# The opening of a two-block kernel by feature columns, with the low part's product of the first projection one chunk later

## The chip, the core and the metric

The kernel runs on one core of one Trainium2 chip. The metric is the device time of one execution in microseconds (us). The engines are TensorE (PE; its weight loads are PEld), VectorE (DVE), ScalarE (ACT), GpSimd (POOL) and SyncE (SP), which here only issues transfers. Each engine works through its own queue in order; between engines there are semaphores.

## What is computed

Two blocks follow each other on x (1 x 1024 tokens x 1024 features, fp32). The first has two layers of attention and SwiGLU with adaLN modulation, the second an SSM and a short convolution. Only the first lines of the first layer matter here:

```python
cond = silu(c)
mod = cond @ ada_w[0] + ada_b[0]
sh1, sc1, g1, sh2, sc2, g2 = split(mod, 6)
h = rmsnorm(x, norm_mix[0]) * (1 + sc1) + sh1
qkv = h @ a_w_in[0]          # 16 query heads, 4 key/value heads of 64
```

`rmsnorm` divides each token by the root of the mean of its squares (plus 1e-6) and multiplies by a gain per feature.

## The kernel before

**The data.** h is kept with features on partitions: eight chunks k of 128 features x 1024 tokens. Every matrix product is split: h and the weight tile are each cut into a high part (fp32r) and a low part (what is left), and a product is three matmuls: high weight x high h (L1500), high weight x low h (L1501), low weight x high h (L1502). A tile of a weight is 128 partitions x 1024. ScalarE makes its high part (`tile_highs`, L2531), VectorE its low part (`tile_lows`, L3592). Attention runs in units; unit 0 needs the three tiles kv, q0 and q1, each for two halves of 512 tokens.

**The opening.** SyncE loads vec, c, the eight token tiles of x (`x_start`, L998), the kv tile and then the adaLN weights of chunk 0 to 7 (`ada_start`, L1003, 1 MB each, six places), with q0 behind chunk 1 and q1 behind chunk 5. ScalarE squares the token tiles with its accumulator (`square_tile`, L2612; VectorE does the last, L3618). VectorE and ScalarE make the factor per token in two groups of four tiles (`factor_of`, `root_of`) and scale x by it, four tiles each (`scale_tile`). TensorE spreads silu(c) over the partitions (L1554), runs 12 spare products (`spare_products`, L1431) and turns x chunk by chunk into PSUM (`turn_x`, L1546), up to three chunks ahead.

**The chunk loop.** For each chunk VectorE takes two products of a 128x1024 adaLN tile with silu(c), summed over the row (`modulation`, L2892), which give shift and scale, then the gain (L3638); ScalarE writes h from the turned x with gain and shift (L2638) and its high part (L2641); VectorE writes the low part of the chunk before (`first_low`, L3630). TensorE's `project_first` waits for that low part (`h_ready`) and runs kv and q0 of the chunk, 12 products; the 48 products of q1 come in one piece behind chunk 7, with the turn of the values (`turn_values`, L1571) ahead of its chunk 6. Then `attention` goes on: VectorE copies keys and values out of PSUM (L3418, L3420), ScalarE the queries, SyncE loads unit 1's kv tile when a place is free (L872), and TensorE alternates scores (L1593) with the projection of unit 1.

**GpSimd** builds identity, distances and the ALiBi tables of units 0 and 1 (`bias_tables`, L1148), and then waits for unit 0's projection to issue adaLN loads (L1162).

The order is written out by hand on each engine. The spare products and the first lines of the projection read:

```python
def spare_products(n, dst=psum[:, 3584:3840]):
    for _ in range(n):
        nc.tensor.matmul(dst, ident[:, :], pick[:, 0:2, :], start=True, stop=True)
```

## Time and profile before

| | us |
|---|---|
| median of 3 runs | 2569.73 (2568.26 to 2569.94) |
| profiled execution, its own time | 2567.95 |
| its span | 2565.9 |
| TensorE busy | 2529.6 (99%) |
| VectorE busy | 1970.2 (77%) |
| ScalarE busy | 1035.0 (40%) |
| GpSimd busy | 321.0 (13%) |

The page gives busy times and a chain of waits. Behind it stand views of the trace: instructions in order of time (merged where equal ones follow each other, so that the second number is the time from the first start to the last end), the chain in order of time, one line's instructions, and busy times by stretch. An fp32 matmul leaves two records, an fp32r one leaves one. Ends of matmuls are modelled, so the time of one is read from start to start.

### The profile page before, as it was taken

What the parts mean: (1) busy time and instruction counts of PE and PEld (TensorE: products, weight loads), DVE (VectorE), ACT (ScalarE), POOL (GpSimd) and SP (SyncE); (2) the same over time, 40 slices, a digit from 0 to 9 for tenths busy, and PEclk for the clock granted to TensorE, in tenths of its full rate; (3) what the DMA queues carried; (4) which work ended last, traced back from release to release, by engine and by line L of the source; (5) the groups of instructions that cost most, each with busy time, mean ns of one, the idle gap of its engine ahead of it and who ended that gap; (6) DMA issues with size and microseconds to landing.
All of it is one profiled execution on the core that took longest, in us unless ns stands there. A gap on an engine that the chain in (4) does not pass through costs nothing.

```text
span 2565.9 us, 37223 instructions
## 1 busy us (share of the span) xinstructions
PE 2529.6 (99%) x12662; PEld 2018.7 (79%) x12662; DVE 1970.2 (77%) x3476; ACT 1035.0 (40%) x1946; POOL 321.0 (13%) x454
## 2 busy tenths in 40 slices
PE   8999999999999999999999999999999999999998
PEld 6666688888888888777776888888888888878987
DVE  7888757889999889845555888998999987433566
ACT  6445725343333333454446453333333343111233
POOL 2011101000000000301111200000000017971000
PEclk9999999999999999999999999999999999999999
DMA  6333231211111111222322112121111132113122
GB/s 239 116 139 124 99 107 54 62 54 61 49 53 53 57 57 45 90 84 94 99 99 108 40 43 62 50 61 57 49 57 55 59 83 74 50 42 60 34 99 82
DMA packets 182017, 192.61 MB, mean 75 GB/s; under 512 B 18353, under 2 KB 146577, under 8 KB 181490
## 3 DMA queue, kind: packets, MB, share of 16 engines
q1 hardware_dynamic: 169954, 147.48, 18.0%
q0 software_dynamic: 11952, 43.65, 5.4%
q8 instruction: 69, 1.13, 0.2%
q14 instruction: 42, 0.34, 0.0%
HBM read 177.34 MB, written 12.58 MB: 74 GB/s over the span
## 4 chain that ended last, share of the span: by engine, by line
PE 93%; DVE 4%; ACT 2%; issue 1%; DMA 1%; POOL 0%; SPq 0%; DVEq 0%
PE psum L1423 21%; PE psum L1730 10%; PE psum L1731 10%; PE psum L1732 10%; PE psum L1500 5%; PE psum L1783 4%; PE psum L1782 4%; PE psum L1786 4%; PE psum L1502 4%; PE psum L1501 4%; PE psum L1771 3%; PE psum L1593 3%; PE psum L1621 3%; PE psum L1605 3%; DVE arena L2892 1%
## 5 line engine op out<-in xcount | busy, mean ns | idle before, releaser
L3181 DVE SCALAR_TENSOR_TENSOR xT<-psum,mod,xT 128x512 f32<-128x512 f32 x504 | 356.4, 745 | 61.6 <-PE psum L1786 61.3
L2346 ACT ACTIVATE w_high<-wpair 128x512 fp32r<-128x512 f32 x240 | 146.5, 626 | 315.8 <-DVE wpair L3113 244.9
L1423 PE MATMUL psum<-hT_high,w_low 128*128 128x512 f32 x928 | 261.0, 392 | 0.2 <-DVE arena L2888 0.2
L2549 ACT ACTIVATE arena<-arena 128x256 f32<-128x256 f32 (+3 forms) x296 | 146.6, 497 | 157.3 <-DVE arena L3451 157.1
L1500 PE MATMUL psum<-hT_high,w_low 128*128 128x512 f32 x480 | 203.0, 423 | 3.4 <-DVE h_low_mix L3630 3.2
L1423 PEld LDWEIGHTS psum<-hT_high,w_low 128*128 128x128 f32 x928 | 172.9, 188 | 38.3 <-issue 2.5
L1502 PE MATMUL psum<-hT_high,w_low 128*128 128x512 f32 x480 | 189.3, 394 | 0.0
L1501 PE MATMUL psum<-h_low_mix,w_low 128*128 128x512 f32 x480 | 188.5, 393 | 0.0
L1732 PE MATMUL psum<-hT_high,w_low 128*128 128x512 f32 x480 | 186.7, 389 | 0.0
L1730 PE MATMUL psum<-hT_high,w_high 128*128 128x512 f32 x472 | 183.6, 389 | 0.0
L1731 PE MATMUL psum<-h_low,w_high 128*128 128x512 f32 x472 | 183.6, 389 | 0.0
L3099 DVE TENSOR_TENSOR w_low<-wpair,w_high 128x512 fp32r<-128x512 f32 x240 | 161.8, 682 | 2.1 <-ACT w_high L2346 1.7
L1223 POOL TENSOR_TENSOR w_high<-arena,w_high 128x512 fp32r<-128x512 f32 x2 | 2.6, 1292 | 1233.9 <-ACT w_high L2333 1233.9
L3592 DVE TENSOR_TENSOR w_low<-wpair,w_low 128x1024 fp32r<-128x1024 f32 x70 | 88.6, 1267 | 85.5 <-ACT w_low L2531 85.4
L1782 PE MATMUL psum<-hT_high,w_low 128*128 128x512 f32 x360 | 140.1, 389 | 0.0
L1423 PE MATMUL psum<-h_low_mix,w_low 128*128 128x512 f32 x448 | 135.3, 390 | 0.2 <-ACT arena L2273 0.2
L1500 PEld LDWEIGHTS psum<-hT_high,w_low 128*128 128x128 f32 x480 | 90.4, 188 | 57.1 <-issue 36.3
L2531 ACT ACTIVATE w_low<-wpair 128x1024 fp32r<-128x1024 f32 x76 | 80.0, 1054 | 130.6 <-DMA wpair<-in_w_in_dram 94.1
L2562 ACT ACTIVATE arena<-psum 128x1024 f32<-128x1024 f32 (+2 forms) x80 | 85.2, 1066 | 87.8 <-PE psum L1605 87.7
L3451 DVE CUSTOM_DVE_ANT_0 arena<-psum,arena 128x192 f32<-128x192 f32 (+2 forms) x180 | 53.8, 353 | 86.0 <-PE psum L1593 86.0
L2392 ACT ACTIVATE arena<-psum 128x512 f32<-128x512 f32 x80 | 47.9, 599 | 170.3 <-PE psum L1732 114.6
L3113 DVE TENSOR_TENSOR wpair<-wpair 128x512 f32<-128x512 f32 x160 | 109.9, 687 | 6.6
(450 smaller groups left out, 6257.5 us busy)
## 6 DMA issues: line engine op xcount, KB each, us to landing
wpair<-in_ffn_w_in_dram SPq DMA_DIRECT2D x176, 256.0 KB, 2.9
wpair<-in_ada_tiles_dram POOLq DMA_DIRECT2D x20, 1024.0 KB, 5.2
arena<-in_ffn_w_out_dram SPq DMA_DIRECT2D x80, 256.0 KB, 2.9
wpair<-in_ada_tiles_dram POOLq DMA_DIRECT2D x32, 512.0 KB, 3.6
wpair<-in_w_in_dram SPq DMA_DIRECT2D x24, 512.0 KB, 3.8
wpair<-in_b_tiles_dram SPq DMA_DIRECT2D x18, 512.0 KB, 3.3
arena<-in_ada_tiles_dram SPq DMA_DIRECT2D x8, 1024.0 KB, 15.6
wpair<-in_a_tiles_dram SPq DMA_DIRECT2D x12, 512.0 KB, 4.6
```

The costliest lines, as they stand in the source:

```text
L1423: mm = nc.tensor.matmul(dst[:, HALF * a:HALF * a + HALF], w(k), src(k)[:, HALF * t:HALF * t + HALF], start=first and n == 0 and w is high ...
L1500: nc.tensor.matmul(dst, high[:, k, :], hT_high[:, k, rows], start=k == 0, stop=False)
L1501: nc.tensor.matmul(dst, high[:, k, :], h_low_mix[:, k, rows], start=False, stop=False)
L1502: mm = nc.tensor.matmul(dst, low[:, k, :], hT_high[:, k, rows], start=False, stop=k == KC - 1)
L1730: nc.tensor.matmul(bank[dst], high[:, k, :], moving_high(k), start=start and k == 0, stop=False, skip_group_check=not start)
L1731: nc.tensor.matmul(bank[dst], high[:, k, :], moving_low(k), start=False, stop=False, skip_group_check=not start)
L1732: mm = nc.tensor.matmul(bank[dst], low[:, k, :], moving_high(k), start=False, stop=k == 3, skip_group_check=not start)
L1782: nc.tensor.matmul(dst, down_high[w][:, cols], hid_high[v], start=start, stop=False, skip_group_check=not start)
L2346: nc.scalar.activation(of_step(s, first_high, part_high)[name], part_raw[name], ACT.Copy).then_inc(part_high_ready, 1)
L2549: e = nc.scalar.activation(s, s, ACT.Exp, bias=stat_n[:, ti, h:h + 1], scale=-1.0, accum_out=stat_l[:, ti, h:h + 1])
L3099: nc.vector.tensor_tensor(part_low[name], part_raw[name], as_f32(high), ALU.subtract).then_inc(part_split, 1)
L3181: nc.vector.scalar_tensor_tensor(xT[:, m, rows], psum[:, HALF * j:HALF * j + HALF], mod[:, l, 40 + m:41 + m], xT[:, m, rows], ALU.mult, AL ...
```

## The change

x is loaded from its transposed copy `x_rows`, which the kernel already had, so features are on partitions from the start (`x_raw`). The turning of x and the scaling by token tile are gone. ScalarE squares each chunk without its accumulator (VectorE half of the last); TensorE sums the squares over features with one-column products (`square_sums`, eight per chunk), 14 spare products follow, then it spreads the factor over partitions (`factor_wide`, `r_spread`), and 26 more spare products. ScalarE copies the spread factor to `r_wide`. GpSimd multiplies each chunk by it (`scaled`; VectorE does half of chunk 0) and also makes the low parts of kv, q0 and q1 of unit 0. ScalarE writes h and its high part both straight from `x_raw`. In the projection both products with the high part of h run first, the one with the low part a chunk later, and q1 of chunks 0 to 4 runs inside the loop. The q1 load stands behind ada chunk 2.

```diff
-            for t in range(ST):
-                sp.dma_start(x_start[:, t, :], x[0, P * t:P * t + P, :]).then_inc(x_moved[t], 16)
+            for k in range(KC):
+                sp.dma_start(x_raw[:, k, :], x_columns[:, k, :]).then_inc(x_moved[k], 16)
...
-                if k in (1, 5):
+                if k in (1, 2):
                     load_mix("q0" if k == 1 else "q1", 0)
...
+            def tile_lows(name):
+                whole, high, low = tile_parts(name)
+                pool.wait_ge(tile_high, SPLITS.index(name) + 1)
+                pool.wait_ge(tile_split, SPLITS.index(name))
+                nc.gpsimd.tensor_tensor(low, whole, as_f32(high), ALU.subtract).then_inc(tile_split, 1)
+            def scaled(k, first=0):
+                pool.wait_ge(x_moved[k], 16)
+                nc.gpsimd.tensor_tensor(x_raw[:, k, first:S], x_raw[:, k, first:S], r_wide[:, first:S], ALU.mult).then_inc(scaled_ready, 1)
...
             bias_tables(0)
+            tile_lows(("kv", 0))
+            pool.wait_ge(r_kept, 2)
+            scaled(0, HALF)
+            scaled(1)
+            tile_lows(("q0", 0))
+            scaled(2)
+            tile_lows(("q1", 0))
+            for k in range(3, KC):
+                scaled(k)
             bias_tables(1)
...
                 for k in range(KC):
-                    if u == 0:
-                        for n in range(k + 2 if k else 0, min(k + 3, KC)):
-                            turn_x(n)
-                    pe.wait_ge(h_ready, h_number(2 * UNITS[u].layer, k))
+                    pe.wait_ge(shifted, shift_number(0, k))
                     for what in ("kv", "q0"):
+                        with_highs(what, k)
+                    for n in ((k - 1, k) if k == KC - 1 else (k - 1,)):
+                        if n >= 0:
+                            pe.wait_ge(h_ready, h_number(0, n))
+                            for what in ("kv", "q0"):
+                                with_lows(what, n)
+                    if 2 <= k < KC - 1:
                         for half in range(2):
-                            project_chunk(u, what, half, k, first_place(what, half))
-                for k in range(KC):
-                    if k == 6:
+                            project_chunk(u, "q1", half, k - 2, first_place("q1", half))
+                for k in range(5, KC):
+                    if k == KC - 1:
                         turn_values(u)
                     for half in range(2):
                         project_chunk(u, "q1", half, k, first_place("q1", half))
...
+            def square_sums(k):
+                pe.wait_ge(x_squared, k + 1 if k < KC - 1 else KC + 1)
                 for t in range(ST):
+                    mm = nc.tensor.matmul(psum[:, 3584 + t:3585 + t], square_place[k % 2][:, P * t:P * t + P], ones[:, :],
+                                          start=first, stop=k == KC - 1, skip_group_check=t > 0)
+                mm.then_inc(first_norm, 1)
...
+            for k in range(KC):
+                square_sums(k)
+            pe.wait_ge(const_ready, 6)
+            spare_products(14, psum[:, 2560:2816])
+            factor_wide()
+            spare_products(26, psum[:, 2560:2816])
...
+                act.wait_ge(x_moved[k], 16)
+                if k >= 2:
+                    act.wait_ge(first_norm, k - 1)
+                nc.scalar.activation(square_place[k % 2][:, first:S], x_raw[:, k, first:S], ACT.Square).then_inc(x_squared, 1)
...
+                act.wait_ge(scaled_ready, k + 1)
+                nc.scalar.activation(xT[:, k, :], x_raw[:, k, :], ACT.Identity, bias=shift_, scale=gain_)
+                nc.scalar.activation(hT_high[:, k, :], x_raw[:, k, :], ACT.Identity, bias=shift_, scale=gain_).then_inc(shifted, 1)
...
+            dve.wait_ge(first_norm, KC - 1)
+            last = x_raw[:, KC - 1, 0:HALF]
+            nc.vector.tensor_tensor(square_place[1][:, 0:HALF], last, last, ALU.mult).then_inc(x_squared, 1)
...
+                    if k == 0 and b == 0:
+                        dve.wait_ge(r_kept, 1)
+                        nc.vector.tensor_tensor(x_raw[:, 0, 0:HALF], x_raw[:, 0, 0:HALF], r_wide[:, 0:HALF], ALU.mult)
...
-                if k == 0:
-                    tile_lows(("kv", 0))
-                else:
+                if k > 0:
                     first_low(k - 1)
-                if k == 1:
-                    tile_lows(("q0", 0))
```

TensorE's queue from the spread of silu(c) (L1554, in the changed kernel L1600) to the first transposes (`turn_x`, L1546), before:

```order
L1554 MATMUL psum<-arena,ones 128x512
L1431 MATMUL psum<-pick,ident 128x256 [waits x_squared,const_ready]
L1431 MATMUL psum<-pick,ident 128x256 x11
L1546 MATMUL psum<-ident,arena 128x128 [waits scaled_ready,cond_ready]
L1546 MATMUL psum<-ident,arena 128x128 x7
```

and now, from the sums of the last chunk (L1583) on, which seven pairs like it precede, to the first projection product (L1533):

```order
L1583 MATMUL psum<-ones,arena 128x1 [waits x_squared]
L1583 MATMUL psum<-ones,arena 128x1 x7
L1447 MATMUL psum<-pick,ident 128x256 [waits const_ready]
L1447 MATMUL psum<-pick,ident 128x256 x13
L1591 MATMUL psum<-ident,rst 128x128 [waits rstd_ready]
L1591 MATMUL psum<-ident,rst 128x128 x7
L1447 MATMUL psum<-pick,ident 128x256 x26
L1533 MATMUL psum<-hT_high,w_low1 128x512 [waits tile_split,shifted,cond_ready]
```

The spread of the factor stands between two runs of spare products, and the first projection product behind both.

GpSimd's queue from the end of the distance tables on, before:

```order
L1134 AFFINE_SELECT arena<-arena 128x384 [waits pool_step]
L1136 AFFINE_SELECT arena<-arena 128x384 [waits pool_step]
L1148 TENSOR_SCALAR arena<-arena 128x384 [waits pool_step]
L1148 TENSOR_SCALAR arena<-arena 128x384 x7
L1162 DMA wpair2<-in_ada_tiles_dram 128x2x1024 [waits proj_ready1]
```

and now (L1150 is `bias_tables`, L1157 `tile_lows`, L1162 `scaled`; rows of L1162 for chunks 4 to 7 follow, then the tables of unit 1):

```order
L1150 TENSOR_SCALAR arena<-arena 128x384 x3
L1157 TENSOR_TENSOR w_low1<-wpair1,w_low1 128x1024 [waits tile_split,tile_high]
L1162 TENSOR_TENSOR arena<-arena 128x512 [waits x_moved0,r_kept]
L1162 TENSOR_TENSOR arena<-arena 128x1024 [waits x_moved1]
L1157 TENSOR_TENSOR w_low0<-wpair0,w_low0 128x1024 [waits tile_split,tile_high]
L1162 TENSOR_TENSOR arena<-arena 128x1024 [waits x_moved2]
L1157 TENSOR_TENSOR w_low2<-wpair2,w_low2 128x1024 [waits tile_split,tile_high]
L1162 TENSOR_TENSOR arena<-arena 128x1024 [waits x_moved3]
```

Eleven tensor_tensor instructions have come in ahead of the tables of unit 1.

## Rows read from the trace of the kernel before

**Rows 1.** Page of the profile, its first line.

```profile
span 2565.9 us, 37223 instructions
```

**Rows 2.** Chain of waits in order of time, the opening: start us, us, what.

```profile
14.56 1.21 DVE xT L3618
...
17.64 0.46 DVE arena L3609
...
19.49 1.20 DVE arena L2892
...
22.10 1.14 DVE w_low L3592
...
45.68 1.13 DVE h_low_mix L3630
...
49.42 1.15 DVE h_low_mix L3630
```

**Rows 3.** Instructions in order of time, TensorE, the opening: start us, us, what.

```profile
3.98 3.75 PE L1554 MATMUL psum<-arena,ones 1*128 1x512 f32 x4 [3.98 <-ACT arena L2603]
...
27.03 0.50 PE L1500 MATMUL psum<-hT_high,w_low 128*128 128x512 f32 x1 [2.54 <-DVE h_low_mix L3630]
...
54.14 0.39 PE L1500 MATMUL psum<-hT_high,w_low 128*128 128x512 f32 x1
...
64.11 0.39 PE L1502 MATMUL psum<-hT_high,w_low 128*128 128x512 f32 x1
...
64.43 0.71 PE L1571 MATMUL psum<-ident,arena 64*128 64x64 f32 x8
...
68.67 0.50 PE L1500 MATMUL psum<-hT_high,w_low 128*128 128x512 f32 x1
```

**Rows 4.** Instructions in order of time, TensorE, the spare products: whole, then two stretches.

```profile
11.67 8.13 PE L1431 MATMUL psum<-pick,ident 128*128 128x256 f32 x24 [3.94 <-ACT arena L2612]
...
12.66 3.62 PE L1431 MATMUL psum<-pick,ident 128*128 128x256 f32 x8
...
17.48 1.89 PE L1431 MATMUL psum<-pick,ident 128*128 128x256 f32 x8
```

**Rows 5.** The line of the spare products, their weight loads: ns min/median/max, first and last start.

```profile
L1431 PEld LDWEIGHTS psum<-pick,ident x62: 186/190/337, 11.6 to 1420.2; 128*128 128x128 f32 x62
```

**Rows 6.** Instructions in order of time, TensorE: a one-column sum in the FFN.

```profile
392.26 0.95 PE L1449 MATMUL psum<-ones,hT 128*128 128x1 f32 x8
```

**Rows 7.** Instructions in order of time, GpSimd: a weight tile's low part.

```profile
1384.07 2.36 POOL L1182 TENSOR_TENSOR w_low<-wpair,w_low 128x1024 fp32r<-128x1024 f32 x1 [3.00 <-ACT w_low L2531]
```

**Rows 8.** Instructions in order of time, GpSimd beside VectorE, single instructions from three stretches.

```profile
8.26 1.18 POOL L1148 TENSOR_SCALAR arena<-arena 128x384 f32<-128x384 f32 x1
...
15.07 1.73 POOL L1148 TENSOR_SCALAR arena<-arena 128x384 f32<-128x384 f32 x1
...
2177.51 0.62 POOL L1356 TENSOR_TENSOR arena<-arena 128x256 f32<-128x256 f32 x1
...
2178.10 1.61 POOL L1357 TENSOR_TENSOR arena<-arena 128x256 f32<-128x256 f32 x1
...
2179.26 1.53 DVE L3844 TENSOR_TENSOR arena<-arena 128x1024 f32<-128x1024 f32 x1
...
2179.79 1.61 POOL L1358 TENSOR_TENSOR arena<-arena 128x256 f32<-128x256 f32 x1
```

**Rows 9.** Instructions in order of time, the end of the opening: VectorE, SyncE, ScalarE.

```profile
54.34 1.40 DVE L3418 COPY arena<-psum 64x512 f32<-64x512 f32 x2
...
57.93 0.69 DVE L3420 COPY arena<-psum 64x512 f32<-64x512 f32 x1
...
56.37 0.82 SPq L872 DMA_DIRECT2D wpair<-in_a_tiles_dram  x2
...
61.42 1.06 ACT L2531 ACTIVATE w_low<-wpair 128x1024 fp32r<-128x1024 f32 x1 [3.95 <-DMA wpair<-in_a_tiles_dram]
```

**Rows 10.** Busy us by stretch: PE, PEld, DVE, ACT, POOL; then granted clock, DMA share, GB/s.

```profile
27.40:30.80 3.40, 3.40 (x10) 2.62 (x9) 3.37 (x7) 0.82 (x2) 0.00 (x0) 0.50 1.02 408
```

More of the change, by code:

```diff
@@ L1175, in half_tile_low @@
                     ins.then_inc(tile_split, 1)
-            def tile_lows(name):
-                whole, high, low = tile_parts(name)
-                pool.wait_ge(tile_high, SPLITS.index(name) + 1)
-                pool.wait_ge(tile_split, SPLITS.index(name))
-                nc.gpsimd.tensor_tensor(low, whole, as_f32(high), ALU.subtract).then_inc(tile_split, 1)
             def sink_difference(t):
@@ L2634, in _ @@
+            for k in range(KC - 1):
+                square_chunk(k)
+            square_chunk(KC - 1, HALF)
+            act.wait_ge(var_ready, 1)
+            nc.scalar.activation(dev[:, 0, :], var[:, 0, :], ACT.Sqrt).then_inc(dev_ready, 1)
             tile_highs(("kv", 0))
+            act.wait_ge(first_norm, KC + 1)
+            for half in range(2):
+                cols = slice(HALF * half, HALF * half + HALF)
+                nc.scalar.activation(r_wide[:, cols], r_spread[:, cols], ACT.Copy).then_inc(r_kept, 1)
```

107 lines of the change are left out of this document (38 added, 69 removed).

## The prediction

> **What bounds the kernel now.** I read the page first: TensorE is busy almost the whole span [rows 1], and the change touches only the opening, so the question is when the opening ends. The mark is the first projection product of attention unit 1, at 68.67 us [rows 3]: everything behind it has the same order in both kernels and moves with it. The chain of waits for the opening [rows 2] shows VectorE as the bound: square sum of the last x tile at 14.56, the factor until 17.64, two scalings, and from 19.49 the eight chunks, two adaLN products of 1.20 and a low part of 1.15 in each, 3.74 us a chunk (the h_low of two chunks start at 45.68 and 49.42). That last one of the chain ends at 50.57. On top come two weight low parts (22.10 is one). The matmul timeline [rows 3] shows TensorE starting on chunk 0 at 27.03 and, behind the last chunk, q1 in one piece up to 68.
>
> **Cost of the square sums and of the way to the factor.** Before, ScalarE and VectorE sum squares with their accumulators and TensorE has no part in it. Now each chunk needs eight one-column fp32 products on TensorE. The nearest row is the one-column sum of the same shape [rows 6]: 8 records (two to an instruction) in 0.95 us, so 0.11 apart. A chunk is 16 records: 1.8 us. That row is from a stretch at the full clock. In the opening the clock is not full: the spare products stand 8 in 3.62 us at 12.66 and 8 in 1.89 us at 17.48 [rows 4], which is 0.43 and 0.216 from start to start, the two levels 1.2 and 2.4 GHz; and their weight loads take up to 337 ns where 190 is usual [rows 5]. A one-column product is nearly all weight load, so at the low level I take twice 0.11: 3.5 us a chunk. Bounds 1.8 and 3.5; I take 3.5, because TensorE came out of the spread row (3.98 to 7.73) still low, and only a stream of wide products brought it up, after 5.5 us (11.67 to about 17.2, 13 records). Whether one-column products would do that no row shows.
>
> Low clock: sums of chunks 0 to 6 from 7.7, 7 x 3.5 = 24.5, to 32.2. VectorE's half square of chunk 7 waits for chunk 6's sums (first_norm 7): about 0.7 and two handovers, 33.0. Sums of chunk 7: 36.5. x itself has landed by 14.5 [rows 2], so x no longer matters. Then 14 spare products stand in TensorE's queue ahead of the spread of the factor: 28 records, 13 slow (5.5) and 15 fast (3.2) = 8.7, to 45.2. They hide the factor chain (15.8 to 17.6 before, about 2.7 with var and root), and cost 6 us beyond it. The spread is 16 records again, a new 128x128 weight load in each; I take the 0.11 of the one-column row, 1.8: **F = 47.0**, when the factor is wide in PSUM. At the full clock from about 13 us on: 1.6 chunks slow, the other 87 records up to chunk 6 in 9.6, to 22.8; 0.9 and 1.8, 25.5; spares 6.0, spread 1.8: F = 33.3.
>
> A rule of the Trainium skill speaks for the second value by another way: "TensorE: Matmul & The Clock Gate", section "LDWEIGHTS (loading the stationary operand)", gives a load as its columns divided by 1.2 GHz, whatever the array's clock. By it a one-column record would cost 0.11 at the low level too, and F would be about 33 again. The 337 against 190 ns [rows 5] speak against it.
>
> **Work behind F without collisions.** r_wide is copied by 0.7, the half multiply takes 0.6, the second adaLN product of chunk 0 with gain 1.35, seven chunks of 3.7 = 25.8, and h_low of chunk 7 ends at F+31.5. The two weight low parts (2.3), five scalings and the q1 low part have left VectorE. TensorE starts at F+11.2, since the 26 spares behind the spread are 52 records of 0.216; ScalarE's first high part is there earlier. The stream of before goes from 54.14 to 64.11 with 44 starts, 0.227 each [rows 3]; 144 products are 32.7, and the turn of the values 0.64: F+44.5. So without collisions TensorE, not VectorE, is the bound.
>
> **The moved work.** GpSimd gets the low parts of kv, q0 and q1 and the scaling of x. A 128x1024 tensor_tensor takes 2.36 there [rows 7], against 1.14 on VectorE. Behind F these are half a one, 1.2, and nine whole ones, 21.3: 22.5 us, and every one, like every adaLN product and h_low of VectorE, reads two tensors in SBUF. The rows show what that does [rows 8]: L1357 takes 1.61 where its like takes 0.62, because VectorE's L3840 runs; L3844 then takes 1.53 for 1.2; L1358 again 1.61. They alternate, one instruction at a time. It holds for the accumulating kind too: L1148 takes 1.73 at 15.07, while L3618 runs, and 1.18 alone. The Trainium skill states this lock in "SBUF — State Buffer", section "Who interferes with whom", and the trace agrees.
>
> So between two VectorE instructions one GpSimd instruction of 2.36 goes in, until the ten are done, about F+35. Nearly all of the 22.5 is added to VectorE's 31.5, but for 1.1 that falls in its own wait: h_low 7 ends at F+53. Played through instruction by instruction with these durations, high part 7 is there at F+51.8. Bounds: 0 and 22.5; I take 21.4. TensorE, with gaps of up to 9 us, has 34 products left behind the high part of 7: eight, four, four, then q1's chunks 5, 6, 7: 7.7 us, from F+53.1 (it is 1.3 behind), and the turn: F+61.4.
>
> **The moved q1.** That q1 runs early is right with no collision, since it fills TensorE's waits; its cover at the end goes, though. Before, 8.1 us of q1 lie between the end of kv/q0 (56.2) and the turn of values at 64.43, and hide three things [rows 9]: VectorE's six copies (54.34 to 58.62, 4.3), the load of the next kv tile (issued at 56.37, high part at 61.42) and its low part. Now kv ends at F+56.2, copies at F+60.5, turn to F+61.2, last q1 chunk to F+62.6, scores 0.64. The kv load is issued at F+56.7, then 5.05 + 1.06 + 1.14 and handovers: F+64.2. That is the mark. The q1 load moved ahead of ada chunk 3 costs 1.3 us of queue and nothing else, since all ada chunks have landed long before F+20. The clock falls in gaps of this kind (0.50 in 27.40 to 30.80, after TensorE stood from 24.4 to 27.03 [rows 10]); 8 to 16 slow products late in the stream are 2 to 3 us, half of it in waits: +0.5 to 1.
>
> **Sum.** Mark: 47.0 + 64.2 + 0.5 = 111.7, against 68.67: +43 us. The profiled execution took 2567.95 (span 2565.9); 2567.95 + 43 = **2611**. The median of the runs is 1.8 higher, inside the error of F.
>
> **Rivals.** (1) *The sums run at the full rate*, by a clock that rises under one-column products or by weight loads that don't slow down: F = 33.3, mark 97.5 + 0.5, +29: 2597. For it: no row shows one-column products failing to raise the clock. Against: rows 5, and the spread row's wide but one-row products that did not raise it. (2) *GpSimd and VectorE collide little* (the adaLN kind slips through): mark F + 47.3 (44.5, and 2.8 for copies and the kv load in the shorter tail), so +25.5 with F = 47.0: 2593, and +12 with F = 33.3: 2580. Against it: rows 8. (3) *Not slower*: the sums keep up with the landing of x because a one-column product without a wide neighbour costs half the row or less. Then chunk 7's sums end at about 17.2, spares 6.0, spread 1.8, F = 25.0; without collisions the mark is 72.3, +3.6: 2572. It decides from F below 26.5; with the lock it is 2588. It needs chunks of (17.2 - 7.7)/8 = 1.2 us, where the fastest row gives 1.8: unlikely. (4) *Faster*, by VectorE's shorter path alone, asks for F under 16.2, when the sums cannot be done.
>
> **Chances.** Slow sums with the lock 0.45 (2607 to 2617); fast sums with it 0.25 (2592 to 2602); slow sums, no lock 0.08; fast sums, no lock 0.06; sums with the landing and lock 0.05; without 0.05; the rest 0.06. The predicted time is the first. A range of 2586 to 2618 takes in the first three and the fifth, 0.83. The likeliest's own is 2603 to 2618. Within 0.2% means 5 us, about what a measurement of this kernel can tell from no change: 0.04; faster 0.02; slower 0.94.
>
> **What would show it.** In the changed profile: 128 one-column records, 3.5 us a chunk at the low level (1.8: rival 1; 1.2: rival 3); the spread ending near 47; GpSimd's scalings 3.5 long instead of 2.36 and VectorE's adaLN products 3.6 instead of 1.28 while they last (rival 2: unchanged); TensorE waiting for ScalarE's high parts of chunks 2 and 3; then the first unit 1 product waiting for its kv low part. The prediction is wrong if the spread ends before 30, or if the chunks keep a 3.7 us step beside GpSimd.

## The result, and the profile after

The changed kernel takes 2608.65 us (median of four runs, 2607.58 to 2610.47), the kernel before 2569.84 in the runs beside it. The ratio is 1.0152, with a 95% interval of 1.0135 to 1.017: slower by 38.8 us. The prediction was 2611, with a range of 2586 to 2618. The profiled run of the changed kernel took 2608.06 (span 2606.3), 40.1 us more than that of the kernel before.

The matmul timeline of the changed kernel's opening, to be laid beside [rows 3] (start, duration, line, tiles, shape, count, idle time before and what ended it):

```profile
4.00 3.75 PE L1600 MATMUL psum<-arena,ones 1*128 1x512 f32 x4 [4.00 <-ACT arena L2650]
7.68 24.05 PE L1583 MATMUL psum<-ones,arena 128*128 128x1 f32 x112
32.59 3.57 PE L1583 MATMUL psum<-ones,arena 128*128 128x1 f32 x16 [0.86 <-DVE arena L3635]
36.03 8.67 PE L1447 MATMUL psum<-pick,ident 128*128 128x256 f32 x28
44.54 1.95 PE L1591 MATMUL psum<-ident,rst 128*128 128x128 f32 x16
...
105.84 0.68 PE L1613 MATMUL psum<-ident,arena 64*128 64x64 f32 x8 [1.13 <-DVE arena L3455]
...
108.67 0.50 PE L1516 MATMUL psum<-hT_high,w_low 128*128 128x512 f32 x1
```

The one-column sums (L1583) fill TensorE without a gap from 7.68 to 31.7, then come the last sums, the 14 spare products and the spread. The spread ends at 46.5; this is F of the prediction. The last row is the mark: 108.67, where it was 68.67 [rows 3]. It moved by 40.0 us, and so did the span (2606.3 - 2565.9 = 40.4). All but 0.4 us of the loss lies in the opening.

The level of TensorE's clock has to be read from the pace here. The granted clock of the profile says 1.00 for the whole stretch from 4 to 57 us, but it says 1.00 in the kernel before too, both from 12.7 to 16.0 and from 17.5 to 19.4, where the same spare products stand 0.43 and 0.216 us apart [rows 4]. So this early in a trace that number does not settle the level. In run 10 below it has already changed, to 0.50, when the last sums run (38.08 to 41.65), and 16 one-column records take the same 3.57 us there. The view by stretches (busy times of PE, PEld, DVE, ACT and POOL, then the granted clock), first of the changed kernel, then of run 10:

```profile
8.00:31.00 23.00, 23.00 (x110) 23.00 (x109) 1.01 (x1) 5.92 (x6) 4.83 (x5) 1.00 1.03 412
...
38.10:41.50 3.40, 3.40 (x16) 3.40 (x16) 0.00 (x0) 0.00 (x0) 0.00 (x0) 0.50 0.00 0
```

VectorE behind F (same columns), where [rows 2] has its chunks:

```profile
62.71 2.17 DVE L3656 SCALAR_TENSOR_TENSOR gain<-mod,vec 128x1 f32<-128x1 f32 x1
64.81 1.21 DVE L3645 TENSOR_TENSOR h_low_mix<-xT,hT_high 128x1024 fp32r<-128x1024 f32 x1
65.94 3.37 DVE L2927 CUSTOM_DVE_ANT_0 arena<-arena,vec 128x1024 f32<-128x1024 f32 x1
...
72.67 2.21 DVE L3656 SCALAR_TENSOR_TENSOR gain<-mod,vec 128x1 f32<-128x1 f32 x1
74.80 1.21 DVE L3645 TENSOR_TENSOR h_low_mix<-xT,hT_high 128x1024 fp32r<-128x1024 f32 x1
...
88.45 1.27 DVE L2927 CUSTOM_DVE_ANT_0 arena<-arena,vec 128x1024 f32<-128x1024 f32 x1
...
97.33 1.23 DVE L3645 TENSOR_TENSOR h_low_mix<-xT,hT_high 128x1024 fp32r<-128x1024 f32 x1 [1.31 <-ACT hT_high L2676]
```

And GpSimd in the same stretch:

```profile
58.22 3.37 POOL L1162 TENSOR_TENSOR arena<-arena 128x1024 f32<-128x1024 f32 x1
61.54 3.32 POOL L1157 TENSOR_TENSOR w_low<-wpair,w_low 128x1024 fp32r<-128x1024 f32 x1
64.83 16.71 POOL L1162 TENSOR_TENSOR arena<-arena 128x1024 f32<-128x1024 f32 x5
81.63 6.42 POOL L1150 TENSOR_SCALAR arena<-arena 128x384 f32<-128x384 f32 x4
```

A modulation product takes 3.37 us while GpSimd scales a chunk and 1.27 once it has stopped; a chunk goes from h_low to h_low in 9.99 us (64.81 to 74.80) instead of 3.74. Three GpSimd instructions, 3.34 us apart, fit into that time, beside four of VectorE: the two products and the gain wait, the h_low right behind the gain does not (1.21). The whole loss can be read from two places, the front up to 46.5 and this pace. Two waits of the changed kernel, summed over its first 110 us, name them (who waited for whom; us in total, times, longest):

```profile
ACT xT L2675 <- DVE gain L3656: 28.9, 7, 7.6
...
DVE arena L3635 <- PE psum L1583: 22.8, 1, 22.8
```

### The profile page after: what moved, and what is told of

Read it like the earlier page. It is cut to its first block, busy times and chain, and to the rows that moved or that the text cites. A ratio compares the mean times of both kernels' runs of the same rounds, so it can differ in the third digit from the quotient of the medians.

```text
span 2606.3 us, 37487 instructions
## 1 busy us (share of the span) xinstructions
PE 2566.1 (98%) x12798; PEld 2054.3 (79%) x12798; DVE 1983.8 (76%) x3463; ACT 1032.1 (40%) x1937; POOL 353.5 (14%) x465
## 3 DMA queue, kind: packets, MB, share of 16 engines
q1 hardware_dynamic: 169954, 147.48, 17.8%
## 4 chain that ended last, share of the span: by engine, by line
PE 93%; DVE 3%; ACT 2%; issue 1%; DMA 0%; DVEq 0%; SPq 0%; POOL 0%
PE psum L1439 21%; PE psum L1772 10%; PE psum L1774 10%; PE psum L1773 10%; PE psum L1516 5%; PE psum L1828 4%; PE psum L1824 4%; PE psum L1825 4%; PE psum L1518 4%; PE psum L1517 4%; PE psum L1813 3%; PE psum L1635 3%; PE psum L1663 3%; PE psum L1647 2%; PE psum L1583 1%; DVE arena L2927 1%
## 5 line engine op out<-in xcount | busy, mean ns | idle before, releaser
L1439 PE MATMUL psum<-hT_high,w_low 128*128 128x512 f32 x928 | 262.2, 393 | 0.2 <-DVE arena L2923 0.2
L1439 PEld LDWEIGHTS psum<-hT_high,w_low 128*128 128x128 f32 x928 | 173.7, 189 | 38.5 <-issue 2.5
L1516 PE MATMUL psum<-hT_high,w_low 128*128 128x512 f32 x448 | 189.3, 423 | 0.2 <-ACT arena L2586 0.2
L1774 PE MATMUL psum<-hT_high,w_low 128*128 128x512 f32 x480 | 186.7, 389 | 0.0
L1518 PE MATMUL psum<-hT_high,w_low 128*128 128x512 f32 x448 | 175.9, 393 | 0.0
L1517 PE MATMUL psum<-h_low_mix,w_low 128*128 128x512 f32 x448 | 175.3, 391 | 0.0
L1824 PE MATMUL psum<-hT_high,w_low 128*128 128x512 f32 x360 | 140.1, 389 | 0.0
L1439 PE MATMUL psum<-h_low_mix,w_low 128*128 128x512 f32 x448 | 135.7, 392 | 0.2 <-ACT arena L2321 0.2
L1516 PEld LDWEIGHTS psum<-hT_high,w_low 128*128 128x128 f32 x448 | 84.1, 188 | 52.0 <-issue 36.8
## 6 DMA issues: line engine op xcount, KB each, us to landing
arena<-in_ada_tiles_dram SPq DMA_DIRECT2D x8, 1024.0 KB, 15.5
```

The source lines that it names most:

```text
L1439: mm = nc.tensor.matmul(dst[:, HALF * a:HALF * a + HALF], w(k), src(k)[:, HALF * t:HALF * t + HALF], start=first and n == 0 and w is high ...
L1516: nc.tensor.matmul(dst, high[:, k, :], hT_high[:, k, rows], start=k == 0, stop=False)
L1517: nc.tensor.matmul(dst, high[:, k, :], h_low_mix[:, k, rows], start=False, stop=False)
L1518: mm = nc.tensor.matmul(dst, low[:, k, :], hT_high[:, k, rows], start=False, stop=k == KC - 1)
L1774: mm = nc.tensor.matmul(bank[dst], low[:, k, :], moving_high(k), start=False, stop=k == 3, skip_group_check=not start)
L1824: nc.tensor.matmul(dst, down_high[w][:, cols], hid_high[v], start=start, stop=False, skip_group_check=not start)
```

## The experiments

My theory after the result: the loss is a sum of two terms, the front (slow sums and the spare products behind them, both ahead of F) and the pace behind F (GpSimd's two-operand work holding up VectorE). The rivals: the sums only fill time that x needs to land; the clock, kept up by spare products, is what counts; GpSimd is late by itself and does not hold anything up; the new order of terms in the projection is part of the loss. Each experiment edits the changed kernel, but for the one that says otherwise. Interval ratios stand against the kernel before.

**1. The sums on VectorE.**

```diff
-            for k in range(KC):
-                square_sums(k)        # TensorE, 8 one-column products a chunk
+            square_sums()             # 8 products, of the finished sum
...
+            for k in range(1, KC - 1):
+                nc.vector.tensor_tensor(total, square_place[0] if k == 1 else total, square_place[k % 2], ALU.add)
```

> The changed kernel, but the squares of the chunks are added up on VectorE (seven additions of 128 x 1024, some 1.2 us each, beside the landing) and TensorE multiplies only the finished sum by the column of ones: 8 products in place of 64. My theory (the one-column products at 0.2145 us a record hold the front of the opening, 24.05 + 3.57 us): the sums are done at about 26 instead of 36.2, the 14 spare products (still 8.7 us) start there, the spread factors are there at 36 to 37 instead of 46.5, and the time falls by about 10 us to 2599 (2597 to 2601). Rival A (the sums only fill time that the landing of x needs anyway): the last square is not there before 33, and the time stays within 2 us of 2608.7. Rival B (the spare products and the clock that they bring are what counts): TensorE, idle until 25 us, is slower through the whole projection, and the time falls by less than 5 us.

Measured: 2604.09 us (2600.89 to 2604.63), ratio 1.0131 (1.0114 to 1.0148), the profiled run 2600.89. VectorE and TensorE in its trace:

```profile
24.01 1.23 DVE L3642 TENSOR_TENSOR xT<-xT,arena 128x1024 f32<-128x1024 f32 x1
...
25.29 3.57 PE L1582 MATMUL psum<-ones,xT 128*128 128x1 f32 x16 [17.52 <-DVE xT L3642]
...
37.00 1.95 PE L1590 MATMUL psum<-ident,rst 128*128 128x128 f32 x16
```

The sums are done at 28.9, not at 26: I had given the 16 remaining records too little, they take the slow 3.57. F is 38.95, 7.5 us earlier than before the edit, and the mark comes at 101.12, also 7.5 us earlier. In the profiled run the time follows (7.2 us). The median gained 4.6 only: the spans of the other three runs lie 2.4 to 3.1 above that of the profiled one, with a mean granted clock of 0.996 to 0.997 where it has 0.998, and in two of them another 0.9 us lies outside the span. So my size, 10, was too large, and the time lies outside my interval (2597 to 2601); the first rival (landing) is out, since the last square was there at 24.0 and not at 33; the second (clock: less than 5 us gained) is not told apart by the median, and needs the next two.

**2. The same kernel as in run 1, without the 14 spare products.** The edit takes one line more out: `spare_products(14, psum[:, 2560:2816])`.

> As the kernel before in this list, and the 14 spare products between the sums and the spread of the factor are left out too. My theory (whatever TensorE does before the factor is there is front, and nothing more): the factor on VectorE is ready some 2.5 us after the sums, at 28.5, the spread of 16 records takes 1.95 us, or about 3.5 at the low clock, so the front is 30.5 to 32 and the time is 15 to 16 us under that of the changed kernel, 2593 (2591 to 2596). Rival (the clock matters more than the place of the front): without these products the clock is low for the spread and the first projection products, and of the 5 us from the spare products more than 3 are lost again: 2597 or more.

Measured: 2598.25 us (2596.49 to 2600.48), ratio 1.0111 (1.0094 to 1.0128); the profiled run 2596.49.

```profile
26.28 3.57 PE L1582 MATMUL psum<-ones,xT 128*128 128x1 f32 x16 [18.57 <-DVE xT L3641]
31.49 3.75 PE L1590 MATMUL psum<-ident,rst 128*128 128x128 f32 x16 [1.64 <-DVE rst L3111]
```

F is 35.2: the spread takes 3.75 us at the low clock where it took 1.95, and still the front is 11.3 us shorter than in the changed kernel. The mark is at 97.38, 11.3 us earlier. The time fell by 10.4 (11.6 in the profiled runs). F was three to five us later than I expected, for the 3.57 and for the last addition, which ended at 26.2 here. The time lies outside my interval (2591 to 2596), in the region of the rival (2597 or more). The mark tells the two apart in part: against run 1 it came 3.7 us earlier (101.12 to 97.38) for 8.45 us of products taken out. The rest is 1.64 us of waiting for the factor, which the products had covered, 1.0 by which the sums began later in this execution, and 1.8 for the slow spread. So the low clock takes back 1.8 us, not more than 3, and the mark still follows F.

**3. The changed kernel without the 14 spare products.**

> The changed kernel without the 14 spare products (8.67 us) between the sums and the spread. The sums end at 36.2, the factor needs some 2.5 us more (square root 36.5 to 37.6, reciprocal behind it). My theory: the spread is done at 41 to 42.5 in place of 46.5 (at the low clock it takes longer than 1.95 us), all behind it moves with it, and the time is 4 to 5 us less, 2604 (2602.5 to 2605). Rival (the clock gained by the spare products pays for them): the time stays within 1.5 us of 2608.7 or rises.

Measured: 2605.44 us (2603.31 to 2606.68), ratio 1.0134 (1.0117 to 1.0151).

```profile
32.63 3.57 PE L1583 MATMUL psum<-ones,arena 128*128 128x1 f32 x16 [0.86 <-DVE arena L3634]
37.85 3.76 PE L1591 MATMUL psum<-ident,rst 128*128 128x128 f32 x16 [1.64 <-DVE rst L3113]
```

F is 41.6, 4.9 us earlier, and the mark is 103.73, 4.9 us earlier; the time fell by 3.2. Behind the mark this run's span has 2500.2 us left (2603.9 - 103.73) where the changed kernel has 2497.6 (2606.3 - 108.67): the rest of the expected gain is lost there, and other runs show that remainder vary between 2497.0 and 2500.5 without a pattern that goes by the edit. The expected 4 to 5 hold for the mark; the time lies just outside my interval. Over runs 1 to 3 and the changed kernel the mark is at F + 62.2, + 62.1, + 62.1 and + 62.2: the front passes to the end one for one.

**4. The changed kernel without the 26 spare products behind the spread.**

> The changed kernel without the 26 spare products (11.39 us) behind the spread. My theory (VectorE with GpSimd sets the pace there, TensorE only waits): front at 46.5 and pace of a chunk unchanged; the clock is low for the first chunks' products, which are hidden; the time changes by less than 1.5 us, 2608.7 (2607.5 to 2610). Rival (TensorE's first products are on the path): they could start 5 us or more earlier, and the time falls by 3 us or more. Rival (these products hold the clock up for the projection): the time rises by 2 us or more.

Measured: 2609.89 us (2607.76 to 2611.86), ratio 1.0153 (1.0136 to 1.017). The mark is 107.68, 1.0 us earlier because F was (the 14 spare products took 7.68 us in this run, not 8.67). Neither rival holds: 11 us of TensorE's work behind F is hidden in full (the mark stays at F + 62.2), and the clock that it holds up is worth nothing that shows.

**5. The changed kernel with its scaling on GpSimd cut to one column.**

```diff
-                nc.gpsimd.tensor_tensor(x_raw[:, k, first:S], x_raw[:, k, first:S], r_wide[:, first:S], ALU.mult).then_inc(scaled_ready, 1)
+                nc.gpsimd.tensor_tensor(x_raw[:, k, first:first + 1], x_raw[:, k, first:first + 1], r_wide[:, first:first + 1], ALU.mult).then_inc(scaled_ready, 1)
```

The values are then not scaled; all waits stay.

> The changed kernel, but each multiplication of a chunk by the factor on GpSimd takes one column in place of 512 or 1024 (the values are then not scaled; every wait and count stays). Theory of contention (GpSimd's two-operand work and VectorE's hold each other up: VectorE's modulation products take 3.38 us in place of 1.15 while it runs): the modulation products beside it take 1.2 us again, the pace of a chunk falls from 6.6 to about 3.8 us, TensorE then sets the end of the projection at 44 to 45 us behind the spread, the last low part is there by 35 us behind it in place of 52, and the mark comes 9 to 12 us earlier: 2598 (2596 to 2600). Rival (latency of GpSimd alone: ScalarE waits for its product, VectorE is merely slow on its own account): modulation products stay over 2 us. Rival (TensorE at its clock is the bound anyway): the time falls by less than 3 us.

Measured: 2592.89 us (2591.61 to 2593.86), ratio 1.0087 (1.007 to 1.0104); 15.8 us less. VectorE and TensorE in its trace:

```profile
52.59 3.39 DVE L2927 CUSTOM_DVE_ANT_0 arena<-arena,vec 128x1024 f32<-128x1024 f32 x1
...
60.51 1.27 DVE L2927 CUSTOM_DVE_ANT_0 arena<-arena,vec 128x1024 f32<-128x1024 f32 x1
...
81.49 1.23 DVE L3645 TENSOR_TENSOR h_low_mix<-xT,hT_high 128x1024 fp32r<-128x1024 f32 x1 [1.31 <-ACT hT_high L2676]
...
46.02 11.39 PE L1447 MATMUL psum<-pick,ident 128*128 128x256 f32 x52
57.05 3.99 PE L1533 MATMUL psum<-hT_high,w_low 128*128 128x512 f32 x16
60.88 1.07 PE L1540 MATMUL psum<-h_low_mix,w_low 128*128 128x512 f32 x4
61.92 2.11 PE L1533 MATMUL psum<-hT_high,w_low 128*128 128x512 f32 x8
```

The modulation products take 1.27 us, except beside a weight low part of GpSimd, which still runs (3.39). The last low part is there 15.8 us earlier (behind the spread: 15.5), and now TensorE has no gap behind the spare products: it sets the end. The mark is at 92.94, F + 46.8. Both rivals are out: a modulation product does not take over 2 us by itself, and TensorE's own length is not what bound the changed kernel. I had taken the gain 4 to 7 us too small.

**6. GpSimd busy at the same places, but only writing.**

```diff
-                nc.gpsimd.tensor_tensor(x_raw[:, k, first:S], x_raw[:, k, first:S], r_wide[:, first:S], ALU.mult).then_inc(scaled_ready, 1)
+                if k > 0:
+                    pool.wait_ge(scaled_ready, k)
+                nc.gpsimd.memset(LAY[0]["bias"][:, 1, :, :], 0.0).then_inc(scaled_ready, 1)
```

Here too the values are not scaled.

> The changed kernel, but each multiplication of a chunk on GpSimd is replaced by a constant written to 1536 columns of a table that is not in use yet (the values are then not scaled): GpSimd is busy some 1.5 to 2 us at each place and writes, but reads nothing. If reading two operands is what makes VectorE wait: modulation products take about 1.2 us beside it, and the time is that of the run without scaling, about 10 us less than the changed kernel, 2598 to 2600. If any access of GpSimd does it: modulation products beside it take 1.15 us plus the length of its write, 2.7 to 3.2 us, and the time falls by less than 5 us.

Measured: 2593.51 us (2592.99 to 2595.41), ratio 1.0091 (1.0074 to 1.0108), the time of run 5 within 0.6 us. GpSimd, and VectorE beside it:

```profile
59.47 7.39 POOL L1164 MEMSET arena<- 128x1536 f32 x5
66.95 6.64 POOL L1150 TENSOR_SCALAR arena<-arena 128x384 f32<-128x384 f32 x4
...
60.61 1.27 DVE L2930 CUSTOM_DVE_ANT_0 arena<-arena,vec 128x1024 f32<-128x1024 f32 x1
...
68.08 1.52 DVE L2930 CUSTOM_DVE_ANT_0 arena<-arena,vec 128x1024 f32<-128x1024 f32 x1
```

From 59.47 to 66.9 GpSimd writes without pause, and VectorE's products take 1.27 as if it were alone. So it is not GpSimd's being busy that costs, nor its writing, but its reading. The Trainium skill says in "SBUF — State Buffer", section "Who interferes with whom", that a VectorE instruction with two SBUF inputs contends with a GpSimd instruction that reads SBUF and not with one that only writes; the trace agrees (1.27 against 3.37). The trace adds a size between, which that rule does not give: beside GpSimd's tensor_scalar (L1150, one operand, 128x384), which reads SBUF too, the product takes 1.52 only.

**7. The scaling on VectorE.**

```diff
-            for k in range(3, KC):
-                scaled(k)             # GpSimd, the other chunks alike
...
-                    if k == 0 and b == 0:
-                        dve.wait_ge(r_kept, 1)
-                        nc.vector.tensor_tensor(x_raw[:, 0, 0:HALF], x_raw[:, 0, 0:HALF], r_wide[:, 0:HALF], ALU.mult)
+                    if b == 0:
+                        dve.wait_ge(r_kept, 2)
+                        nc.vector.tensor_tensor(x_raw[:, k, :], x_raw[:, k, :], r_wide[:, :], ALU.mult).then_inc(scaled_ready, 1)
```

> The changed kernel with the multiplication of every chunk by the factor on VectorE (8 of 128 x 1024, 1.15 to 1.2 us each) and none on GpSimd, which keeps the three low parts of the weights. Theory of contention: VectorE gets 9 us more work but loses some 15 to 20 us of waiting; its pace is 4.9 to 5 us a chunk against 6.6, the last low part is there 42 to 46 us behind the spread in place of 52, and the time falls by 6 to 10 us: 2601 (2598.5 to 2603). Rival (VectorE's own work is the bound, and the contention costs little): the time rises, or falls by less than 2 us.

Measured: 2602.44 us (2601.81 to 2604.03), ratio 1.0123 (1.0106 to 1.014): 6.2 us less. VectorE was given eight instructions of 1.22 us in place of half a one, and is done earlier: the last low part ends at 92.1 instead of 98.6, and the mark is at 101.50, F + 54.9, 7.2 us earlier. The rows of one chunk without GpSimd:

```profile
69.99 1.27 DVE L2921 CUSTOM_DVE_ANT_0 arena<-arena,vec 128x1024 f32<-128x1024 f32 x1
...
71.20 1.22 DVE L3648 TENSOR_TENSOR arena<-arena 128x1024 f32<-128x1024 f32 x1
72.33 1.27 DVE L2921 CUSTOM_DVE_ANT_0 arena<-arena,vec 128x1024 f32<-128x1024 f32 x1
...
73.65 0.16 DVE L3650 SCALAR_TENSOR_TENSOR gain<-mod,vec 128x1 f32<-128x1 f32 x1
73.73 1.22 DVE L3639 TENSOR_TENSOR h_low_mix<-xT,hT_high 128x1024 fp32r<-128x1024 f32 x1
```

Their step is 4.87 us. The same multiplication took 2.1 us of VectorE's time when GpSimd did it and 1.14 when VectorE did.

**8. The order of terms alone, in the kernel before.** The opening stays; in the first projection the waits and products go `with_highs(k)`, then `with_lows(k - 1)`, as in the changed kernel, for keys, values and q0 (q1 stays in one piece behind them).

> The kernel before with one part of the change alone: in the first projection of keys, values and the first queries the two terms of a chunk's high part come first and the low part's term one chunk later; the opening by token tiles stays. My theory: of the 12 products of the last chunk that wait for its low part (0.227 us each), 8 are done by then, so the time falls by about 1.8 us: 2568.0 (2567 to 2569). If this order were a part of the loss of the changed kernel, the time would rise by 2 us or more. If TensorE is the bound there through all chunks, it stays within 0.7 us of 2569.8.

Measured: 2569.17 us (2567.42 to 2571.34, ten runs) against 2571.15 for the kernel before in the thirteen runs beside it; ratio 0.9994, interval 0.9984 to 1.0003. The interval runs from 4.1 us less to 0.8 us more: it cannot tell my 1.8 us from nothing, but it rules out the 2 us more that would make this order a part of the loss. The matmul timeline shows what became of the 1.8 us:

```profile
52.67 2.12 PE L1517 MATMUL psum<-hT_high,w_low 128*128 128x512 f32 x8 [0.71 <-ACT hT_high L2662]
...
64.69 0.71 PE L1592 MATMUL psum<-ident,arena 64*128 64x64 f32 x8
```

The turn of the values comes at 64.69, in the kernel before at 64.43 [rows 3]. In the kernel before, TensorE idled 0.70 us for the low part of a chunk:

```profile
50.60 0.50 PE L1500 MATMUL psum<-hT_high,w_low 128*128 128x512 f32 x1 [0.70 <-DVE h_low_mix L3630]
```

Now it idles 0.71 for the high part of chunk 7. In both, TensorE is full from this last wait to the mark. The stretch behind the wait is 1.81 us shorter (50.60 to 68.67 before, 52.67 to 68.93 now), which is the 8 products. But the last wait ends 2.07 us later. Of that, 0.87 is only that VectorE's loop ran later in this execution (its last low part starts at 52.65, before at 51.78). The other 1.2 belongs to the new order: the wait is for chunk 7's high part now, and was for chunk 6's low part. So by these rows some 0.6 us of my 1.8 is left, an estimate that no median here can show. The order of terms by itself is no part of the loss.

**9. Three repairs together: sums and scaling on VectorE, no 14 spare products.**

> The changed kernel with the three repairs together: the squares added up on VectorE, no 14 spare products ahead of the spread, and the multiplication by the factor on VectorE. My theory (front of the opening and pace of the chunks are two terms that add up): the spread ends at 35.2 us as in the run without spare products, the mark is 55 us behind it as in the run with the scaling on VectorE, so it comes at 90.3 instead of 108.7: the time is 18 us under the changed kernel, 2590.5 (2588.5 to 2593), and still 20 us over the kernel before. Rival (one limit hides the other: with an earlier front VectorE or a load is the bound, or the low clock at the front costs more): less than 14 us, 2595 or more. Rival (the design as such is sound once repaired): the kernel before is reached, 2572 or less.

Measured: 2592.42 us (2588.83 to 2592.87), ratio 1.009 (1.0073 to 1.0106); the profiled run 2588.83.

```profile
31.39 3.69 PE L1584 MATMUL psum<-ident,rst 128*128 128x128 f32 x16 [1.64 <-DVE rst L3105]
...
90.01 0.50 PE L1510 MATMUL psum<-hT_high,w_low 128*128 128x512 f32 x1
```

The mark was expected at 90.3 and is at 90.01; F is 35.1. The repairs of run 2 (11.3) and run 7 (7.2) make 18.5 together, measured 18.7: the two terms add up. The time fell by 16.2 and lies within my interval.

**10. The 14 spare products ahead of the sums.** This is for the first rival of the prediction (sums at the full rate).

```diff
+            spare_products(14, psum[:, 2560:2816])
             for k in range(KC):
                 square_sums(k)
-            spare_products(14, psum[:, 2560:2816])
```

> The changed kernel with the 14 spare products moved ahead of the one-column sums, where TensorE waits for the first chunks anyway, so that the clock can be high when the sums begin. Theory A (a one-column record takes 0.2145 us only because the clock is low, and the sums let the clock fall again by themselves): the first sums run at some 0.107 us a record, the granted clock falls within the sums, the later ones are at 0.2145; the spread ends at 38 to 41, 5.5 to 8 us earlier, and the time falls to 2601 to 2603. Theory B (the sums hold the clock once it is high): all chunks' sums take 1.7 us, they keep up with the landing, the spread ends at 30 to 34, and the time falls by 12 us or more. Theory C (the record's length does not go by the clock): 0.2145 us at the high clock too, sums end at 36 or later as before, and the time falls by at most the spare products' 6 us.

Measured: 2607.89 us (2607.44 to 2611.38), ratio 1.0149 (1.0132 to 1.0165): no gain, where theory A asked for 2601 to 2603. But the records say what was asked. The instructions of the sums from 15.8 to 17.9 us, and from 18.2 to 31.4 (durations in ns, least, median and most), and behind them the same two stretches in the view by stretches (the number behind the busy times is the granted clock):

```profile
L1583 PEld LDWEIGHTS psum<-ones,arena x20: 190/192/192, 15.7 to 17.8; 128*128 128x128 f32 x20
...
L1583 PEld LDWEIGHTS psum<-ones,arena x64: 192/333/333, 18.1 to 31.3; 128*128 128x128 f32 x64
```

```profile
15.80:17.90 2.10, 2.10 (x22) 2.10 (x20) 0.00 (x0) 0.25 (x1) 0.00 (x0) 1.00 1.02 408
18.20:31.40 13.20, 13.20 (x65) 13.20 (x64) 0.00 (x0) 4.59 (x5) 0.00 (x0) 0.50 1.02 408
```

The clock was at 2.4 GHz when the sums began, behind 8 us of spare products; then a record came every 0.11 us. At about 18.1 us, with nothing but one-column records since 15.7, it fell to 1.2 GHz, and from there a record came every 0.213 us. So theory A of this run holds for the mechanism: the rate goes by the clock, and the sums cannot hold it. For the size I was wrong: in the changed kernel the sums had not idled, they began at 7.7. Here they begin 8.0 us later, win 2.5 of it back (21.51 us for the first seven chunks instead of 24.05), and end at 41.65 instead of 36.2. The 8.67 us of spare products saved behind them are used up by these 5.5 us, by 1.54 us of waiting for the factor, and by the spread at the low clock (3.78 instead of 1.95): F is 46.98, 0.5 us later than in the changed kernel. The mark of the profiled execution, the longest of the four, is at 110.46, F + 63.5. That is 1.3 more than in the runs above: chunk 4's products run at the low clock from 86.0 on (granted clock 0.57 from 86 to 90, where the changed kernel has 1.00 from 85.5 to 89.9), and behind them TensorE has no gap that could hide it. The Trainium skill ("TensorE: Matmul & The Clock Gate", "LDWEIGHTS (loading the stationary operand)") gives the time of a load as its columns over 1.2 GHz, with no term for the array's clock; the measured 192 and 333 ns for the same shape decide against that.

**11. Repaired kernel, and five modulation products ahead of the spread.**

```diff
+            early_products([(0, 0), (0, 1), (1, 0), (1, 1)])   # ahead of the variance
...
             reciprocal_root(0).then_inc(rstd_ready, 1)
+            early_products([(2, 0)])
```

> The kernel with the three repairs, and five of VectorE's sixteen modulation products (those of chunks 0 and 1, one of chunk 2) moved ahead of the spread: four into VectorE's idle 3.7 us ahead of the variance, one behind the factor. Theory (what is left between this kernel and the one before is VectorE's loop over the chunks, which starts when the factor is there and not when the first modulation tile is): three to four products of 1.2 us leave the loop, some 1 us is added to the front, and the time falls by 2.5 to 4 us against 2592.4: 2589 (2588 to 2590.5). Rival (TensorE is the bound behind the spread, 4.1 us a chunk and 11 us of spare products ahead of them): less than 1 us.

Measured: 2588.31 us (2586.04 to 2588.69), ratio 1.0069 (1.0052 to 1.0086). The mark is at 86.43, 3.6 us earlier than in run 9, and the time is 4.1 less. VectorE's loop sets the end there still (a step of 4.88 us, TensorE waits 0.5 us in each chunk). It is the fastest kernel of this design that ran, and 18 us slower than the kernel before.

## Why the prediction was right, step by step

**The place of the loss.** Right: the opening up to the mark; behind it 2497.6 us of the span remain, 2497.2 before (2565.9 - 68.67).

**Slow sums.** Right, and the largest step: 3.5 us a chunk forecast, 3.41 measured (ScalarE's squares, each of which waits for a chunk's sums, start 3.41 us apart; from one record to the next that is 0.213. The 0.2145 in my expectations is 24.05 us over 112 records, with the end of the last one in it). Sums up to chunk 6 were forecast to end at 32.2 and ended at 31.7; the half square began at 31.85; last sums forecast to 36.5, measured 36.2. The bet for 3.5 against 1.8 was decided by one doubt, whether one-column products bring the clock up. They did not in 24 us, and run 10 shows the clock falling under them. The fast-sum rival (0.25) had the right price of a record (0.11 in run 10 at the high clock), but its condition did not hold; its F of 33.3 was reached by no run with the sums on TensorE.

**Spare products and spread.** 8.7 forecast, 8.67 measured; spread 1.8, measured 1.95. F = 47.0 forecast, 46.5 measured. The cost that I gave the 14 spares beyond the factor chain, 6 us, was 4.9 (run 3), since without them the spread runs slow (3.76).

**GpSimd against VectorE.** Right in kind: VectorE's product 3.6 forecast, 3.37 measured; GpSimd's 3.5 forecast, 3.32 to 3.37 measured; done at F + 35, measured 81.5 = F + 35.0. VectorE's loss: 21.4 forecast, 20.0 measured, from the sums by line of the stretch from 47 to 100 us:

```profile
L2927 DVE CUSTOM_DVE_ANT_0 arena<-arena,vec 128x1024 f32<-128x1024 f32 x15 | 32.8, 2219 | 0.0
...
L3656 DVE SCALAR_TENSOR_TENSOR gain<-mod,vec 128x1 f32<-128x1 f32 x8 | 7.7, 964 | 0.3
```

15 products at 1.28 would be 19.2, so 13.6 lost; 8 gains at 0.16 would be 1.3, so 6.4 lost. Here the step had a hole: I did not name the gain instruction, one column wide, as one that waits too. It takes 2.2 us where 0.16 is its own time, in three of eight chunks. And I let one GpSimd instruction in between any two of VectorE's; the h_low behind the gain never took longer for it (1.21 to 1.23 in every chunk). The total came out since I counted GpSimd's instructions and not VectorE's, so this part of the agreement is partly luck. The last low part was to end at F + 53 and ended at F + 52.1.

**Without collisions TensorE is the bound.** Right as a rival's condition: forecast mark F + 47.3, run 5 gives F + 46.8. GpSimd's scaling is therefore worth 15.4 us at the end (62.2 - 46.8); the part of the 20.0 us that its low parts of the weights cost VectorE was taken away by no run, and TensorE, without a gap in run 5, would not let it show.

**The tail.** Mis-sized by 2 us, and by the wrong chain. Keys and values were to be done at F + 56.2; the first copy started at 101.41, F + 54.9. The load of the next kv tile was taken at 5.05 us from issue to high part [rows 9] and took 3.87 (issued 102.02, high part at 105.89; why it was shorter no run shows). The prediction let this load and its low part end last, and named TensorE's wait for that low part as a sign. The sign did not come: TensorE has no idle time between the turn of the values (105.84) and the mark. What binds is the other chain of the prediction, which it had at F + 63.2: VectorE's six copies, which end at 105.7, the turn of the values, the last q1 chunk and the scores.

```profile
105.00 0.69 DVE L3455 COPY arena<-psum 64x512 f32<-64x512 f32 x1
106.56 0.69 DVE L3464 COPY arena<-psum 128x512 f32<-128x512 f32 x1 [0.86 <-PE psum L1613]
107.17 1.22 DVE L3625 TENSOR_TENSOR w_low<-wpair,w_low 128x1024 fp32r<-128x1024 f32 x1
```

The turn waits 1.13 us for the copy (the row at 105.84 further up), and the mark follows its start by 2.83. The load varies from run to run, from issue to high part from 3.5 us in run 6 (86.37 to 89.91) to 3.9 in run 11 (79.77 to 83.71), and the mark stays at the start of the turn + 2.83 in all runs from 1 to 7 and 9 to 11 (0.01 more or less). The kv low part starts behind VectorE's copy of the values in all of them and ends 0.28 or 0.29 before the mark: near, but it holds nothing up. F + 64.2 was forecast, F + 62.2 measured; with 0.5 less in F and 0.5 that I had set aside for the clock, these are the 3.0 us between 111.7 and 108.67. The first copy was early because chunk 7's high part was there at 97.30, F + 50.8 (forecast F + 51.8), and TensorE, which last waits at 85.46 and is full from there on, came to it 0.9 behind, not 1.3.

**The clock in the gaps.** Right in sign: the granted clock is 0.50 from 64.75 to 71.55 and from 78.45 to 81.80, behind gaps in which TensorE waits for high parts. It costs nothing there, as all of those products stand ahead of the next wait; in run 10, where the clock was low one gap later, it cost 1.3 us.

**The order of terms.** The prediction gave it no term of its own in the sum but called the early q1 right, "since it fills TensorE's waits". Run 8 shows the reordering of the terms at no difference that can be told; q1 ahead of the end was not tried by itself in the kernel before, because there its place in PSUM is in use.

**What is left.** That the repaired kernel (run 11) stays 17.8 us behind at the mark was not taken apart by a run. Its rows and those of before give an account: VectorE's loop starts at 36.2 instead of 19.5 (+16.7), five products of 1.2 are out of it (-6.0), eight scalings of 1.14 in (+9.1), two weight low parts out (-2.3), GpSimd's remaining low parts and tables hold it up by some 5.3, and it waits 1.2 for one high part: +24.0, and its last low part ends 24.0 us later (77.0 against 53.0). The mark follows 9.4 us behind it instead of 15.7, as q1 has been done. So the factor that must be ready before any chunk can start is what the design costs; this is argued from rows, not shown.

## What to carry to other kernels

A reduction over partitions by one-column products does not cost by its columns: at the low clock a record of one column took 0.213 us, one of 256 columns 0.43, and TensorE's weight loads filled the stretch from 8 to 31 us. Such a stream did not bring the clock up here and did not hold it in run 10: price it at the low level, and look whether an idle VectorE can add the tiles first. Work moved to GpSimd is not off VectorE's account when both read two operands from SBUF. In this kernel 1.14 us of VectorE's work became 2.1 us of VectorE's waiting. And products moved away from the end count only as far as the last wait ahead of them stays where it was: in run 8, by its rows, 0.6 of 1.8 us.

## What the runs showed that I had not expected

- A one-column instruction of VectorE (128x1, 0.16 us) takes 2.2 us beside GpSimd's two-operand work, 2 us more than alone. A small instruction is held up as long as a large one. But the 128x1024 h_low right behind it is not held up at all (1.21), so VectorE's loss goes by the number of GpSimd instructions that are let in, three in a chunk, not by the number of its own.
- One-column records kept TensorE busy in every slot for 24.05 us and the distance of the records stayed 0.213; in run 10 the clock fell from 2.4 to 1.2 GHz under them, though TensorE never paused.
- GpSimd writing 128x1536 in 1.48 us (7.39 for five) costs VectorE nothing; beside its one-operand table work (128x384) a product takes 0.24 us more, beside its two-operand work (128x1024) 2.1.
- The time behind the mark, where all these variants are alike, differs by up to 3.5 us between their profiled executions (2497.0 to 2500.5). For edits of the opening the mark in the trace tells more than the median.
